# Gate weights split once: the first span stores both halves in DRAM, the other four load them

## The chip, the cores and the metric

One core of one Trainium2 chip runs the whole program. The metric is the device time of one execution in microseconds (us). The program is a hand-scheduled kernel: every engine has its own instruction stream, and semaphores tie the streams together.

## The reference

One inference step of a one-layer hybrid decoder, for 2048 prompt positions and 8 x 4 sample positions, all in float32. What bears on the change is the first half of the layer:

```
xn = rmsnorm(x, g_mix)
proj = xn @ w_in                     # 1024 x 4360
mq, mk, mv, mo, mi, mf, aq, ak, av, gt = split(proj)
h_m = mlstm(...) * sigmoid(mo)       # mo: 512 columns
h_a = sliding_window_attention(...)
ga, gb = split(sigmoid(gt))          # gt: 2048 columns
x = x + (ga * (h_m @ w_a) + gb * (h_a @ w_b)) @ w_out
```

`mo` and `gt` together are 2560 columns, which is 20 tiles of 128 columns of weights. These 20 tiles are "the gate weights" here.

## The kernel before

The program has three phases: the projection of everything that the mixers need, the mixing (`mixer_phase`, lines 462 to 1750), and the merge with the FFN (`ffn_phase`). The change lies in the mixing alone.

**What the mixing does.** It walks over 17 chunks (16 prompt chunks of 128 positions and the sample chunk, which comes first) and computes mLSTM and attention for each. These are many small, dependent operations. Between them TensorE (PE) works through the gate products: the 2080 positions are cut into 5 spans of 416 (`SPANS`, `TB`), and each span is multiplied with the 20 weight tiles (`SGN`). One such product is a *unit*; there are 100 (`GUNITS`), numbered u = 20 b + i for span b and tile i.

**A unit.** Float32 products are made of two float32r parts. The raw weight tile (128 x 1024, 512 KB) is loaded into `raw[u % 3]` (`unit_load`). ScalarE (ACT) rounds it into `wh[u % 3]` (`unit_high`, L764), VectorE (DVE) writes the residual `wl[u % 3]` (`unit_low`, L770), and PE does 24 matmuls, wh x xh, wh x xl and wl x xh for 8 row tiles, into the PSUM bank `pp[u % 2]` (`units_pe`, L829). ACT copies the bank to `gsgo[u % 2]` (`unit_act`, L750), and SyncE (SP) stores that to DRAM (`unit_store`, L639). So before the change every weight tile is loaded raw and split five times, once for each span.

**What sets the order.** PE does a unit in two halves of 12 matmuls. A fixed table, `PLACES`, says which halves stand between which pieces of a chunk: 1, 3, 1, 1, 2, 1 and 2 halves in the seven places of an ordinary chunk, so 5.5 units. ACT, DVE and SP walk the same table. All streams are in order: an instruction that waits holds back all that stand behind it.

**The waits around a unit.** PE waits for `gw_lo` (tile split) and for `g_read` (bank of unit u - 2 copied out). ACT waits, before it copies out unit u, for the store of unit u - 2 (`sg_out`), since both use the same buffer. SP issues every DMA of this phase, all on one queue:

```
def units(n, k):
    for u, h in PLACES[n][k]:
        if h == 0:
            continue
        unit_load(u + GRAWS)        # waits: tile u split
        unit_store(u - 2)           # waits: unit u - 2 copied out
```

Between these, in order, SP also loads the rows of the next chunk (`rows_load`, L606 and L607), the chunk's maxima (L615), stores the mixed rows (L674), loads the next span of x (L620), and at chunk 9 a block of loads for the phase that follows (`ahead`, L689 to L707).

Of the kernel before, what the change touches and what calls it, by code (L numbers as in the profile page):

```python
# [6 lines left out]
F32 = mybir.dt.float32  # L7
# [5 lines left out]
P = 128  # L13
D = 1024
KT = D // P
# [418 lines left out]
SGN = MO + 2 * KT  # L434
GUNITS = SPANS * SGN
GRAWS, GWS = 3, 3
# [25 lines left out]
def mixer_phase(nc, a, scratch, ctx, ev, sb, pb, next_ev):  # L462

    def wait(engine, name, count):

        if not (isinstance(count, int) and count <= 0):
            engine.wait_ge(ev(name), count)
# [1 line left out]
    N, S = CHUNKS + 1, 1  # L469
    row_of = lambda n: n - 2 if n > S else CHUNKS  # L470
    xns, prs, hhs, sgs = scratch["normed"], scratch["rows"], scratch["mixed"], scratch["gates"]
    mxs = scratch["maxima"]
    low, high = scratch["low"], scratch["high"]
    at = [0]

# [67 lines left out]
    wh = [sb(f"gwh{i}", [P, KT * P], F32R) for i in range(GWS)]  # L543
    wl = [sb(f"gwl{i}", [P, KT * P], F32R) for i in range(GWS)]
# [31 lines left out]
    def cupped(engine, n):  # L576

        if n == S:
            engine.wait_ge(ev("cup_s"), SEQS)
        else:  # L580
            wait(engine, "cup", n - 1)
# [8 lines left out]
    def _(sp):  # L590
        def rows_load(n):
            if n > N:
                return
            q = (n - 1) % 2
            wait(sp, "kw_ready", n - 2)
            wait(sp, "qk_tr", n - 2)
            cupped(sp, n - 2)
            if n == S + 2:
                sp.wait_ge(ev("sk_out"), 32)
            wait(sp, "rot_done", n - 2)  # L600
            wait(sp, "vr_ready", n - 2)
            for dst, c0, w in ((qk[q][:], 0, 512), (va[q][:, :, 0:DV], 512, 512), (ar[q][:], 1024, 776)):
                src = prs[row_of(n)][:, c0:c0 + w]
                if c0 == 512:
                    src = src.rearrange("p (h d) -> p h d", h=MH)
                sp.dma_start(dst, src).then_inc(ev(f"rows_in{q}"), 16)  # L606
            sp.dma_start(rope[q][:], a["rope"][row_of(n)]).then_inc(ev(f"rows_in{q}"), 16)  # L607
# [10 lines left out]
        def span_load(b):  # L618
            wait(sp, "gx_lo", KT * b)
            sp.dma_start(xst, xns[:, :, TB * b:TB * b + TB]).then_inc(ev("gx_in"), 16)  # L620

        def unit_load(u):
            if u >= GUNITS:
                return
            b, i = u // SGN, u % SGN
            wait(sp, "gw_lo", u - GRAWS + 1)
            dst = raw[u % GRAWS]
            if i < MO:
                sp.dma_start(dst.rearrange("p (k c) -> p k c", k=KT), a["w_mix"][:, :, C_MO + P * i:C_MO + P * i + P]
                             ).then_inc(ev(f"gw_in{u % GRAWS}"), 16)  # L630
            else:
                sp.dma_start(dst, a["w_gate"][(i - MO) // 2, (i - MO) % 2]).then_inc(ev(f"gw_in{u % GRAWS}"), 16)

        def unit_store(u):
            if u < 0:
                return
            wait(sp, "g_read", u + 1)
            done = next_ev("late_gates") if u >= GUNITS - 2 else ev(f"sg_out{u % 2}")
            sp.dma_start(sgs[u // SGN, u % SGN], kept(u)).then_inc(done, 16)  # L639

        def units(n, k):
            for u, h in PLACES[n][k]:
                if h == 0:
                    continue
                unit_load(u + GRAWS)
                unit_store(u - 2)
                if u % SGN == 4 and u // SGN + 1 < SPANS:
                    span_load(u // SGN + 1)
# [4 lines left out]
        sp.wait_ge(ev("last_rows"), 16)  # L653
        sp.dma_start(gz[:], prs[:, :, 1792:1800].rearrange("n p c -> p n c")).then_inc(ev("gz_in"), 16)
        rows_load(S)
        units(0, 0)
        sp.dma_start(sink[:], a["a_sinks"].partition_broadcast(P)).then_inc(ev("par_in"), 16)
        sp.dma_start(kc, a["cache_k"]).then_inc(ev("kc_in"), 16)
        sp.wait_ge(ev("m_ready"), 1)
        sp.dma_start(m0[0:SAMP, :], a["state_m"]).then_inc(ev("m0_in"), 16)  # L660
        units(0, 1)
        units(0, 2)
        for h in range(MH):
            r = DK * (h % 2)
# [92 lines left out]
            act.activation(xh[:, k, :], xst[:, k, :], ACT.Copy).then_inc(ev("gx_hi"), 1)  # L757

    def unit_high(act, u):
        if u >= GUNITS:  # L760
            return
        act.wait_ge(ev(f"gw_in{u % GRAWS}"), 16 * (u // GRAWS + 1))
        wait(act, "gmm", 2 * (u - GWS + 1))
        act.activation(wh[u % GWS][:], raw[u % GRAWS], ACT.Copy).then_inc(ev("gw_hi"), 1)  # L764

    def unit_low(dve, u):
        if u >= GUNITS:
            return
        wait(dve, "gw_hi", u + 1)
        dve.tensor_tensor(wl[u % GWS][:], raw[u % GRAWS], wh[u % GWS][:].bitcast(F32), ALU.subtract  # L770
                          ).then_inc(ev("gw_lo"), 1)
# [33 lines left out]
    def first_half_pe(pe, h):  # L805

        wait(pe, "gw_hi", 1)
        for w, x, ready in ((wh, xh, "gx_hi"), (wh, xl, "gx_lo"), (wl, xh, None)):
            if w is wl:
                wait(pe, "gw_lo", 1)  # L810
            for j in range(KT // 2 * h, KT // 2 * (h + 1)):
                if ready:
                    wait(pe, ready, j + 1)
                mm = pe.matmul(pp[:, 0, 0:TB], w[0][:, j * P:j * P + P], x[:, j, :],
                               start=(j == 0 and w is wh and x is xh), stop=(j == KT - 1 and w is wl))
        mm.then_inc(ev("gmm"), 1)

    def units_pe(pe, n, k):
        for u, h in PLACES[n][k]:
            if u == 0:  # L820
                first_half_pe(pe, h)
                continue
            wait(pe, "gw_lo", u + 1)
            wait(pe, "g_read", u - 1)
            for j in range(KT // 2 * h, KT // 2 * (h + 1)):
                if u % SGN == 0:
                    wait(pe, "gx_lo", KT * (u // SGN) + j + 1)
                for w, x in ((wh, xh), (wh, xl), (wl, xh)):
                    mm = pe.matmul(pp[:, u % 2, 0:TB], w[u % GWS][:, j * P:j * P + P], x[:, j, :],  # L829
                                   start=(j == 0 and w is wh and x is xh), stop=(j == KT - 1 and w is wl))  # L830
            mm.then_inc(ev("gmm"), 1)
# [845 lines left out]
    @block.scalar  # L1677
    def _(act):
        unit_high(act, 0)
        for h in range(2):  # L1680
            span_high(act, 0, h)
# [81 lines left out]
SGN = MO + 2 * KT  # L1763
# [1255 lines left out]
def build(nc, a):  # L3019

    scratch = {
        "normed": nc.dram_tensor("xn_rows", [P, KT, (CHUNKS + 1) * P], F32).ap(),
        "rows": nc.dram_tensor("proj_rows", [CHUNKS + 1, P, WROW], F32).ap(),
        "mixed": nc.dram_tensor("mixer_rows", [P, KT, SEQ + SAMP], F32).ap(),
        "maxima": nc.dram_tensor("chunk_maxima", [CHUNKS, MH * P], F32).ap(),
        "gates": nc.dram_tensor("gate_rows", [SPANS, SGN, P, TB], F32).ap(),
        "x_res": nc.dram_tensor("x_rows", [P, KT, SEQ + SAMP], F32).ap(),
        "x_norm": nc.dram_tensor("xn_ffn_rows", [P, KT, SEQ + SAMP], F32).ap(),
        "up_parts": nc.dram_tensor("up_parts", [FT, 4, 2, P, QUAD], F32).ap(),
        "down_parts": nc.dram_tensor("down_parts", [len(PARTS) * KT, 2, P, QUAD], F32).ap(),  # L3030
    }

    def events_of(tag):

        events = {}

        def ev(name):
            if name not in events:
                events[name] = nc.alloc_semaphore(tag + name)
            return events[name]  # L3040

        return ev, events

    (ev_a, all_a), (ev_m, all_m), (ev_f, _) = (events_of(t) for t in ("a_", "m_", "f_"))

    def phase(program, ev, next_ev):

        with ExitStack() as ctx:  # L3048
            program(nc, a, scratch, ctx, ev, lambda n, s, d=F32: ctx.enter_context(nc.sbuf_tensor(n, s, d)),
                    lambda n, s: ctx.enter_context(nc.psum_tensor(n, s, F32)), next_ev)  # L3050

    with ExitStack() as outer:
        for name, width in (("low", 2 * KT * TB), ("high", HIGH), ("ghd", MO)):
            scratch[name] = outer.enter_context(nc.sbuf_tensor("both_" + name, [P, width], F32))
        phase(project_phase, ev_a, ev_m)
        nc.clear_and_free_semaphores(list(all_a.values()))
        nc.all_engine_barrier()
        phase(mixer_phase, ev_m, ev_f)
        nc.clear_and_free_semaphores(list(all_m.values()))
        nc.all_engine_barrier()  # L3060
        phase(ffn_phase, ev_f, None)
# [78 lines left out]
```

## Time and profile before

| | us |
|---|---|
| median of 3 runs | 2862.28 |
| lowest and highest run | 2859.83, 2863.77 |
| the profiled execution: its own time | 2858.3 |
| the profiled execution: its span, first to last instruction | 2856.5 |
| PE matmul busy in the span | 2764.0 (97%) |
| DVE busy | 1747.3 (61%) |
| ACT busy | 1323.3 (46%) |
| HBM read, written | 415.33 MB, 152.02 MB |

The mixing runs from about 350 to 1018 us of the span. "Busy" of PE is the union of its matmuls, whose ends are modelled and overlap. The DMA share is the mean busy share of the core's 16 DMA engines; over the span they move 199 GB/s. A wait is put down to what released it.

### The profile page before, as it was taken

The numbers are of one execution on the slowest core, as the hardware profiler recorded it, in microseconds if no ns is written. First come the engines' busy times: TensorE is split into PE (matmuls) and PEld (weight loads), VectorE is DVE, ScalarE is ACT, GpSimd is POOL, SyncE is SP. The second block draws the span as 40 slices with busy tenths as digits, with TensorE's granted clock in tenths as the row PEclk, the third lists the DMA queues.
The fourth block names the chain that finished last, engine by engine and source line by source line (L and its number), as shares of the span: only waits on it lengthen the run. The fifth ranks groups of instructions, "written<-read, shape, count | busy, mean of one in ns | idle before, by whom it ended". The sixth has DMA issues, their size and how long they took to land. (4 is left out here: it accounts for less than half of the span.)

```text
span 2856.5 us, 47085 instructions
## 1 busy us (share of the span) xinstructions
PE 2764.0 (97%) x17306; PEld 2646.6 (93%) x17306; DVE 1747.3 (61%) x2752; ACT 1323.3 (46%) x2520; POOL 431.2 (15%) x663
## 2 busy tenths in 40 slices
PE   8999999999999999999989999999999999999997
PEld 8888799989998989999989999999999998999997
DVE  5212167676767668877887777856544456445554
ACT  4212235454555445555655444773443366333442
POOL 2111021211112222222200000020000003001112
PEclk9999999999999999999999999999999999999998
DMA  5534266556655458777676666767665566755654
GB/s 186 195 128 144 89 206 189 187 161 217 215 165 162 134 201 254 258 265 259 219 281 208 211 212 221 252 204 250 203 200 172 188 204 198 244 185 188 205 194 120
DMA packets 373684, 569.44 MB, mean 199 GB/s; under 512 B 50578, under 2 KB 197586, under 8 KB 373458
## 3 DMA queue, kind: packets, MB, share of 16 engines
q1 hardware_dynamic: 371346, 566.31, 60.3%
q8 instruction: 141, 2.31, 0.3%
q14 instruction: 85, 0.70, 0.1%
q10 hardware_dynamic: 2112, 0.13, 0.0%
HBM read 415.33 MB, written 152.02 MB: 199 GB/s over the span
## 5 line engine op out<-in xcount | busy, mean ns | idle before, releaser
L2376 PE MATMUL f_ps<-f_xt,f_wh 128*128 128x348 f32 (+1 forms) x3696 | 670.6, 324 | 18.8 <-DVE both_high L2805 12.0
L2376 PEld LDWEIGHTS f_ps<-f_xt,f_wh 128*128 128x128 f32 x3696 | 604.9, 190 | 25.0 <-DVE both_high L2805 16.7
L2719 DVE TENSOR_TENSOR f_wl<-both_high,f_wh 128x512 fp32r<-128x512 f32 (+1 forms) x494 | 357.1, 736 | 203.8 <-ACT f_wh L2469 200.1
L2469 ACT ACTIVATE f_wh<-both_high 128x512 fp32r<-128x512 f32 (+1 forms) x494 | 298.8, 621 | 339.6 <-PE f_ps L2381 265.2
L2376 PE MATMUL f_ps<-f_gbuf,f_wh 128*128 128x348 f32 (+1 forms) x2112 | 383.6, 322 | 14.3 <-ACT f_ps L2582 6.3
L2381 PE MATMUL f_ps<-f_xt,f_wl 128*128 128x348 f32 (+1 forms) x1848 | 371.0, 323 | 0.0
L2376 PEld LDWEIGHTS f_ps<-f_gbuf,f_wh 128*128 128x128 f32 x2112 | 342.5, 188 | 19.9 <-ACT both_low L2587 10.0
L2381 PEld LDWEIGHTS f_ps<-f_xt,f_wl 128*128 128x128 f32 x1848 | 309.3, 189 | 0.0
L829 PE MATMUL pp<-gxh,gwh 128*128 128x416 f32 x792 | 290.9, 367 | 1.5 <-DVE gxl L778 1.3
L829 PE MATMUL pp<-gxh,gwl 128*128 128x416 f32 x792 | 279.4, 353 | 0.0
L829 PE MATMUL pp<-gxl,gwh 128*128 128x416 f32 x792 | 278.1, 351 | 0.0
L2381 PE MATMUL f_ps<-f_gbuf,f_wl 128*128 128x348 f32 (+1 forms) x1056 | 214.5, 321 | 0.0
L2920 DVE TENSOR_TENSOR both_low<-f_ps,both_low 128x348 f32<-128x348 f32 (+1 forms) x224 | 114.2, 516 | 160.3 <-PE f_ps L2381 159.6
L2381 PEld LDWEIGHTS f_ps<-f_gbuf,f_wl 128*128 128x128 f32 x1056 | 176.1, 188 | 0.0
L2946 POOL TENSOR_TENSOR f_oc<-both_high,both_low 128x2 f32<-128x2 f32 (+1 forms) x176 | 52.4, 310 | 794.5 <-DVE both_high L2805 602.7
L770 DVE TENSOR_TENSOR gwl<-both_low,gwh 128x1024 fp32r<-128x1024 f32 x100 | 122.6, 1227 | 68.5 <-ACT gwh L764 68.5
L829 PEld LDWEIGHTS pp<-gxh,gwh 128*128 128x128 f32 x792 | 149.0, 188 | 15.0 <-issue 6.9
L2820 DVE SCALAR_TENSOR_TENSOR both_high<-both_high,both_low 128x696 f32<-128x696 f32 (+2 forms) x176 | 129.4, 756 | 41.3 <-ACT both_high L2596 41.2
L829 PEld LDWEIGHTS pp<-gxl,gwh 128*128 128x128 f32 x792 | 149.8, 189 | 1.6
L829 PEld LDWEIGHTS pp<-gxh,gwl 128*128 128x128 f32 x792 | 149.0, 188 | 1.6
L2596 ACT ACTIVATE both_high<-both_high,both_low 128x696 f32<-128x696 f32 (+2 forms) x176 | 137.7, 814 | 1.0 <-DVE both_high L2811 1.0
L2824 DVE SCALAR_TENSOR_TENSOR both_high<-both_high,both_low 128x696 f32<-128x696 f32 (+2 forms) x176 | 129.9, 759 | 4.7
(342 smaller groups left out, 4441.8 us busy)
## 6 DMA issues: line engine op xcount, KB each, us to landing
both_high<-in_w_up SPq DMA_DIRECT2D x220, 256.0 KB, 4.2
f_wh<-up_parts SPq DMA_DIRECT2D x176, 256.0 KB, 2.7
f_wl<-up_parts SPq DMA_DIRECT2D x176, 256.0 KB, 3.0
both_low<-in_w_gate SPq DMA_DIRECT2D x80, 512.0 KB, 4.6
up_parts<-f_wh SPq DMA_DIRECT2D x88, 256.0 KB, 2.9
up_parts<-f_wl SPq DMA_DIRECT2D x88, 256.0 KB, 3.4
both_high<-in_w_br SPq DMA_DIRECT2D x40, 512.0 KB, 4.7
both_high<-in_w_out SPq DMA_DIRECT2D x40, 512.0 KB, 4.5
```

What stands on the lines that cost most here:

```text
L770: dve.tensor_tensor(wl[u % GWS][:], raw[u % GRAWS], wh[u % GWS][:].bitcast(F32), ALU.subtract).then_inc(ev("gw_lo"), 1)
L829: mm = pe.matmul(pp[:, u % 2, 0:TB], w[u % GWS][:, j * P:j * P + P], x[:, j, :], start=(j == 0 and w is wh and x is xh), stop=(j == KT - 1 ...
L2376: pe.matmul(out, cut(wh, k), x(k), start=(start and k == 0 and x is xhi), stop=False, skip_group_check=not start or not stop)
L2381: mm = pe.matmul(out, cut(wl, k), xhi(k), start=False, stop=(stop and k == K - 1), skip_group_check=not start or not stop)
L2469: act.activation(ring_slot(wh, e, w), src, ACT.Copy).then_inc(ev("w_hi"), 1)
L2596: ins = act.activation(o, t, ACT.Identity, bias=taps[:, f, 4 * s + 3:4 * s + 4], scale=taps[:, f, 4 * s + 2:4 * s + 3])
L2719: dve.tensor_tensor(ring_slot(wl, e, w), src, ring_slot(wh, e, w).bitcast(F32), ALU.subtract).then_inc(ev("w_lo"), 1)
L2820: ins = dve.scalar_tensor_tensor(o, t, tap(1), o, ALU.mult, ALU.add)
L2824: ins = dve.scalar_tensor_tensor(o, t, tap(0), o, ALU.mult, ALU.add)
L2920: dve.tensor_tensor(t, ps[BANK[v][s]][:, 0:w], t, ALU.add).then_inc(ev(f"ps_read{BANK[v][s]}"), 1)
L2946: return pool.tensor_tensor(dst, src, unit.to_broadcast(list(src.shape)), ALU.mult)
```

## The change

In span 0 (units 0 to 19) everything is done as before, and SP also stores wh and wl of each unit, 512 KB each, to a new DRAM tensor `gate_parts` (`halves_out`). From unit 20 on there is no raw load, no rounding on ACT and no residual on DVE: SP loads both halves from `gate_parts` straight into the rings `wh` and `wl` (`halves_load`), which are still three deep. New waits: ACT's rounding of unit u from 3 to 19 waits until both halves of unit u - 3 have been stored; SP waits, before it loads unit u + 2, until PE has finished unit u - 1; PE waits on two load semaphores in place of `gw_lo`.

```diff
--- before.py
+++ after.py
@@ -469,7 +469,7 @@
     N, S = CHUNKS + 1, 1
     row_of = lambda n: n - 2 if n > S else CHUNKS
     xns, prs, hhs, sgs = scratch["normed"], scratch["rows"], scratch["mixed"], scratch["gates"]
-    mxs = scratch["maxima"]
+    mxs, gps = scratch["maxima"], scratch["gate_parts"]
     low, high = scratch["low"], scratch["high"]
     at = [0]
 
@@ -619,8 +619,28 @@
             wait(sp, "gx_lo", KT * b)
             sp.dma_start(xst, xns[:, :, TB * b:TB * b + TB]).then_inc(ev("gx_in"), 16)
 
+        def halves_out(u):
+
+            if u >= SGN:
+                return
+            sp.wait_ge(ev("gw_lo"), u + 1)
+            for j, t in enumerate((wh, wl)):
+                sp.dma_start(gps[u, j], t[u % GWS][:].bitcast(F32)).then_inc(ev(f"half_out{u % GWS}"), 16)
+
+        def halves_load(u):
+
+            if u < SGN or u >= GUNITS:
+                return
+            v = u - GWS
+            sp.wait_ge(ev("gmm"), 2 * (v + 1))
+            sp.wait_ge(ev(f"half_out{u % SGN % GWS}"), 32 * (u % SGN // GWS + 1))
+            if v < SGN:
+                sp.wait_ge(ev(f"half_out{v % GWS}"), 32 * (v // GWS + 1))
+            for j, (t, name) in enumerate(((wh, "hi_in"), (wl, "lo_in"))):
+                sp.dma_start(t[u % GWS][:].bitcast(F32), gps[u % SGN, j]).then_inc(ev(f"{name}{u % GWS}"), 16)
+
         def unit_load(u):
-            if u >= GUNITS:
+            if u >= SGN:
                 return
             b, i = u // SGN, u % SGN
             wait(sp, "gw_lo", u - GRAWS + 1)
@@ -643,6 +663,8 @@
                 if h == 0:
                     continue
                 unit_load(u + GRAWS)
+                halves_out(u + 1)
+                halves_load(u + GWS - 1)
                 unit_store(u - 2)
                 if u % SGN == 4 and u // SGN + 1 < SPANS:
                     span_load(u // SGN + 1)
@@ -653,6 +675,7 @@
         sp.wait_ge(ev("last_rows"), 16)
         sp.dma_start(gz[:], prs[:, :, 1792:1800].rearrange("n p c -> p n c")).then_inc(ev("gz_in"), 16)
         rows_load(S)
+        halves_out(0)
         units(0, 0)
         sp.dma_start(sink[:], a["a_sinks"].partition_broadcast(P)).then_inc(ev("par_in"), 16)
         sp.dma_start(kc, a["cache_k"]).then_inc(ev("kc_in"), 16)
@@ -757,14 +780,16 @@
             act.activation(xh[:, k, :], xst[:, k, :], ACT.Copy).then_inc(ev("gx_hi"), 1)
 
     def unit_high(act, u):
-        if u >= GUNITS:
+        if u >= SGN:
             return
+        if u >= GWS:
+            act.wait_ge(ev(f"half_out{u % GWS}"), 32 * (u // GWS))
         act.wait_ge(ev(f"gw_in{u % GRAWS}"), 16 * (u // GRAWS + 1))
         wait(act, "gmm", 2 * (u - GWS + 1))
         act.activation(wh[u % GWS][:], raw[u % GRAWS], ACT.Copy).then_inc(ev("gw_hi"), 1)
 
     def unit_low(dve, u):
-        if u >= GUNITS:
+        if u >= SGN:
             return
         wait(dve, "gw_hi", u + 1)
         dve.tensor_tensor(wl[u % GWS][:], raw[u % GRAWS], wh[u % GWS][:].bitcast(F32), ALU.subtract
@@ -820,7 +845,12 @@
             if u == 0:
                 first_half_pe(pe, h)
                 continue
-            wait(pe, "gw_lo", u + 1)
+            if u < SGN:
+                wait(pe, "gw_lo", u + 1)
+            else:
+                n = len([x for x in range(SGN, u + 1) if x % GWS == u % GWS])
+                pe.wait_ge(ev(f"hi_in{u % GWS}"), 16 * n)
+                pe.wait_ge(ev(f"lo_in{u % GWS}"), 16 * n)
             wait(pe, "g_read", u - 1)
             for j in range(KT // 2 * h, KT // 2 * (h + 1)):
                 if u % SGN == 0:
@@ -3026,6 +3056,7 @@
         "gates": nc.dram_tensor("gate_rows", [SPANS, SGN, P, TB], F32).ap(),
         "x_res": nc.dram_tensor("x_rows", [P, KT, SEQ + SAMP], F32).ap(),
         "x_norm": nc.dram_tensor("xn_ffn_rows", [P, KT, SEQ + SAMP], F32).ap(),
+        "gate_parts": nc.dram_tensor("gate_parts", [SGN, 2, P, KT * P], F32).ap(),
         "up_parts": nc.dram_tensor("up_parts", [FT, 4, 2, P, QUAD], F32).ap(),
         "down_parts": nc.dram_tensor("down_parts", [len(PARTS) * KT, 2, P, QUAD], F32).ap(),
     }
```

On SP, at the start of the mixing, from the raw load of unit 4 on (`in_w_mix` and `in_w_gate` are raw weight tiles, `gsgo` is a copied-out unit), there stood:

```order
L632 DMA both_low<-in_w_gate 128x1024
L657 DMA sink<-in_a_sinks 128x8
L658 DMA both_high<-in_cache_k 128x1024
L660 DMA m<-in_state_m 32x4
L632 DMA both_low<-in_w_gate 128x1024
L639 DMA gate_rows<-gsgo 128x416
```

and now:

```order
L652 DMA both_low<-in_w_gate 128x1024
L628 DMA gate_parts<-gwh 128x1024
L628 DMA gate_parts<-gwl 128x1024
L680 DMA sink<-in_a_sinks 128x8
L681 DMA both_high<-in_cache_k 128x1024
L683 DMA m<-in_state_m 32x4
L652 DMA both_low<-in_w_gate 128x1024
L628 DMA gate_parts<-gwh 128x1024
L628 DMA gate_parts<-gwl 128x1024
L659 DMA gate_rows<-gsgo 128x416
```

The two pairs of stores of halves here are those of units 2 and 3; those of units 0 and 1 stand just above, so eight stores now stand ahead of the first store of a result (`gate_rows<-gsgo`). The state, cache and row loads follow behind it as they did.

On SP in an ordinary chunk of a later span, from the load of the next chunk's rows on, there stood:

```order
L606 DMA qk<-proj_rows 128x512
L606 DMA va<-proj_rows 128x4x128
L606 DMA ar<-proj_rows 128x776
L607 DMA rope<-in_rope 128x128
L615 DMA am<-chunk_maxima 128x512
L674 DMA mixer_rows<-ht 1024x1x128
L632 DMA both_low<-in_w_gate 128x1024
L639 DMA gate_rows<-gsgo 128x416
```

and now:

```order
L606 DMA qk<-proj_rows 128x512
L606 DMA va<-proj_rows 128x4x128
L606 DMA ar<-proj_rows 128x776
L607 DMA rope<-in_rope 128x128
L615 DMA am<-chunk_maxima 128x512
L697 DMA mixer_rows<-ht 1024x1x128
L640 DMA gwh<-gate_parts 128x1024
L640 DMA gwl<-gate_parts 128x1024
L659 DMA gate_rows<-gsgo 128x416
```

One raw load for each unit has become two loads of halves. They stand directly ahead of the store of a result, as the raw load did.

## Rows read from the trace of the kernel before

**Rows 1.** the page: span; PE and the DMA engines in 40 slices
```profile
span 2856.5 us, 47085 instructions
...
PE   8999999999999999999989999999999999999997
...
DMA  5534266556655458777676666767665566755654
```

**Rows 2.** windows of the mixing: busy us per engine, PEclk, DMA share, GB/s
```profile
350.00:490.00 140.00, 135.56 (x984) 125.79 (x985) 93.81 (x228) 66.01 (x145) 24.28 (x26) 0.96 0.65 207
390.00:420.00 30.00, 29.27 (x283) 27.41 (x282) 21.16 (x72) 8.45 (x19) 6.54 (x8) 0.94 0.19 53
420.00:490.00 70.00, 68.78 (x488) 63.59 (x488) 46.54 (x86) 36.24 (x86) 8.49 (x8) 1.00 0.69 213
490.00:1000.00 510.00, 501.90 (x3479) 460.75 (x3478) 361.42 (x627) 262.18 (x603) 101.27 (x98) 1.00 0.55 176
```

**Rows 3.** rounding and residual: count, ns min/median/max, first and last start
```profile
L764 ACT ACTIVATE gwh<-both_low x100: 1040/1049/1062, 350.6 to 999.4; 128x1024 fp32r<-128x1024 f32 x100
...
L770 DVE TENSOR_TENSOR gwl<-both_low,gwh x100: 1209/1218/1599, 354.2 to 1003.1; 128x1024 fp32r<-128x1024 f32 x100
```

**Rows 4.** waits of PE, 490 to 1000 us: line, for whom, total us, times, longest us
```profile
PE p L1111 <- DVE hm L1236: 3.2, 8, 1.1
PE p L1101 <- ACT pt L1299: 1.4, 1, 1.4
PE pp L829 <- DVE gxl L778: 1.3, 2, 0.8
PE p L1040 <- DVE sm L1174: 1.3, 1, 1.3
PE p L1088 <- DVE sm L1192: 0.8, 1, 0.8
```

**Rows 5.** windows in three stretches of full queues (columns as in rows 2)
```profile
370.00:380.00 10.00, 9.79 (x61) 8.73 (x59) 6.28 (x28) 6.18 (x12) 0.00 (x0) 1.00 1.05 318
380.00:390.00 10.00, 10.00 (x79) 9.45 (x78) 5.07 (x15) 3.94 (x10) 3.40 (x4) 1.00 0.92 361
710.00:720.00 10.00, 10.00 (x71) 9.09 (x70) 7.47 (x12) 2.88 (x4) 5.59 (x7) 1.00 1.05 402
```

**Rows 6.** DMA issues, 348:1025, last row 350:390: count, KB, us to landing
```profile
both_low<-in_w_gate SPq DMA_DIRECT2D x80, 512.0 KB, 4.6
...
gate_rows<-gsgo SPq DMA_DIRECT2D x98, 208.0 KB, 3.5
...
gate_rows<-gsgo SPq DMA_DIRECT2D x5, 208.0 KB, 7.8
```

**Rows 7.** timeline, first burst: start, us, engine, line [idle before <-releaser]
```profile
362.73 0.33 SPq L639 DMA_DIRECT2D gate_rows<-gsgo  x1
...
370.60 0.52 ACT L750 ACTIVATE gsgo<-pp 128x416 f32<-128x416 f32 x1 [4.05 <-DMA gate_rows<-gsgo]
...
372.60 0.61 ACT L1254 ACTIVATE qkt<-p 128x512 f32<-128x512 f32 x1
...
373.26 0.72 PE L1014 MATMUL p<-qkt 64*128 64x128 f32 x8 [0.21 <-ACT qkt L1254]
```

**Rows 8.** timeline, second burst
```profile
442.71 0.43 SPq L639 DMA_DIRECT2D gate_rows<-gsgo  x1
...
447.68 0.52 ACT L750 ACTIVATE gsgo<-pp 128x416 f32<-128x416 f32 x1 [1.97 <-DMA gate_rows<-gsgo]
...
450.83 1.02 ACT L1299 ACTIVATE pt<-p 128x1024 f32<-128x1024 f32 x1
...
451.90 1.09 PE L1101 MATMUL p<-pt,var 128*64 128x128 f32 x16 [1.05 <-ACT pt L1299]
```

**Rows 9.** timeline, three units apart: last matmul of unit 60, first of unit 63
```profile
760.83 0.35 PE L829 MATMUL pp<-gxh,gwl 128*128 128x416 f32 x1
...
772.76 0.35 PE L829 MATMUL pp<-gxh,gwh 128*128 128x416 f32 x1
```

## The prediction

> **What bounds the kernel now.** I read the page first. PE's matmuls cover 97% of a span of 2856.5 us, and in the slices of the mixing, from the fifth to the fifteenth, its digit is 9 nearly everywhere [rows 1]. So work taken off ACT and DVE can gain only where PE stands waiting for them. The DMA engines have digits of 4 to 7 over most of the span, which looks like room. But a slice is 71 us long and hides bursts.
>
> The windows show them [rows 2]. In 490 to 1000 us (spans 1 to 4) PE is busy for 501.9 of 510.0 us and the DMA share is 0.55. In 350 to 490 us (span 0) the share is 0.65, and it is uneven: 0.19 in 390 to 420. Taking that and 420 to 490 away leaves 0.65 x 140 - 0.19 x 30 - 0.69 x 70 = 91.0 - 5.7 - 48.3 = 37.0 us busy in the 40 us from 350 to 390. There the queue is full already, as the windows of 10 us say: shares 1.05 and 0.92 at 318 and 361 GB/s [rows 5].
>
> What a full queue does to PE is in the first timeline [rows 7]. The store of unit 0's result is issued at 362.73. ACT stands idle for 4.05 us until it has landed at 370.60, since unit 2 goes into the same buffer. Behind that copy, in ACT's order, stand a rounding and the copies for the sample chunk, the last of them at 372.60, and PE's L1014 at 373.26 has waited 0.21 us for that copy. So at this place PE has no slack against the DMA queue. The second timeline is the same pattern [rows 8]: a store issued at 442.71, ACT released by it at 447.68, the copy of the attention weights at 450.83, and PE idle for 1.05 us before L1101. A rule to carry along: before asking what a change frees, ask at which places PE already hangs on the queue that the change loads.
>
> **The change, part by part.**
>
> *Rounding and residual, removed 80 times each.* 80 x 1.049 = 83.9 us of ACT and 80 x 1.218 = 97.4 us of DVE go [rows 3]. Neither engine is the bound, so the gain is at most what PE waits for them in 490 to 1000: 3.2 + 1.4 + 1.3 + 1.3 + 0.8 = 8.0 us [rows 4]. All five groups have ACT or DVE as releaser, but each waits for a chain that also holds work that stays. I take 5 us gained, with 0 and 8 as ends.
>
> *Traffic.* A pair of halves is 2 x 524,288 B = 1.05 MB. Span 0 stores 20 pairs, 21.0 MB. Spans 1 to 4 load 80 pairs, 83.9 MB, in place of 80 raw tiles, 41.9 MB. The best window moved 402 GB/s [rows 5], so I price a pair at 1.05 / 0.40 = 2.6 us of all 16 engines, and the 20 stores at 52.4 us. The Trainium skill, "DMA: Bandwidth & Descriptors", section Specifications, gives some 358 GB/s as the limit of one core against its HBM. By that page the stores would take 58.6 us and my sum would come out about 6 us higher; the 402 GB/s that this trace shows over 10 us (in rows 5) speaks against it as a ceiling, so I do not use it.
>
> *Span 0 as a whole.* The queue is busy for 91.0 us of 140. With the stores, and 1.3 us for two pairs that replace three raw tiles at the end, it is 91.0 + 52.4 + 1.3 = 144.7 us. That no longer fits, even with perfect packing, and packing is poor since SP issues in order.
>
> *First burst, 350 to 390.* Eight stores of halves now stand ahead of the store of unit 0, 4.2 MB or 10.5 us of queue. Some 3 us of room was left (40 - 37.0), so about 8 us arrive at ACT and, by rows 7, at PE. The lower end is 3 us: only the pair of unit 3 stands directly ahead of that store. The upper end is 13 us: that pair also has to wait for the split of unit 3, whose raw tile now lands one pair later. I take 8, since the row it hangs on has no slack. The later stores in this burst fall under a PE that is itself 8 us late, and the queue is nearly empty in 390 to 420 (0.19), where the backlog can drain. I cost them at nothing; if that cover is gone, the result of unit 1 is late next.
>
> *Second burst, 420 to 490.* 48.3 us busy now; ten more pairs (units 10 to 19) and the 1.3 us make 48.3 + 26.2 + 1.3 = 75.8 us in 70. So at least 5.8 us. The upper end is 16: four pairs (units 10 to 13, 10.5 us) ahead of the store in rows 8, which has no slack either, and 5.8 us after it. I take 10.
>
> *Loads of halves in spans 1 to 4.* The ring is three deep and has no raw buffer before it any more. SP may issue the pair of unit u + 2 only when PE has finished unit u - 1, so the pair has the time that PE spends on units u and u + 1. The shortest such time that I found is the one from the end of unit 60, 760.83 + 0.35 = 761.18, to 772.76: 11.6 us [rows 9]. A raw tile of 512 KB lands after 4.6 us [rows 6]; a second one adds 1.3 us of transfer, and two issues some 0.8 us, so 6.7 us. That leaves 4.9 us. A load of x for the next span (1.7 MB, 4.3 us) just fits in. The block at chunk 9 (`ahead`) does not: 4.6 MB, 11.4 us of queue, in which the share is 1.05 already [rows 5]. I take 2 us, between 0 and 8 (one such block with the whole lateness on PE).
>
> *Stores of results in spans 1 to 4.* The store of unit u - 2 stands behind the pair of unit u + 2, so it is issued when PE has finished unit u - 1, and ACT needs it landed when PE has finished u. It lands after 3.5 us [rows 6] plus 2.6 us behind the pair plus the issues: 6.9 us. A unit takes at least 24 x 0.19 = 4.5 us, so ACT stands for up to 2.4 us where two units follow each other directly, once in two chunks. Its rounding of 1.05 us is gone there. Queued behind it is the copy of the attention weights for which L1101 waits. I take 1 us in all, from 0 to 7 (1 us in each of seven pairs of chunks).
>
> *PE's new waits.* Two load semaphores in place of one: they are satisfied in advance or they are the lateness costed above. Nothing more.
>
> **Sum.** -5 + 8 + 10 + 2 + 1 = +16 us. The profiled execution took 2858.3 us, so 2874.3. It lies 4.0 us under the median of 2862.28; in medians that is 2878.3, **2878 us**, slower by 0.55%. With all terms at their low ends the sum is -8 + 3 + 5.8 = +0.8, with all at the high ends +44. They will not all fall on one side: 2864 to 2897 is this case's own range.
>
> What a measurement can tell from no change is 0.2%, 5.7 us: faster is under 2856.6, slower over 2868.0.
>
> **Rivals.**
>
> *Faster: the queue takes the stores in passing (16%).* PE does not wait for halves to be stored, only ACT's rounding three units later does, and 390 to 420 is nearly empty. If the first burst costs PE less than 1 us and the second less than 1 us, the relief of 8 us stands alone: 2862 - 8 + 1 = 2855. It decides at L1014: it holds if the store of unit 0 is not more than 1 us later than now. Against it: rows 7 and 5.
>
> *No change (13%).* The bursts cost their low ends, 3 + 5.8, and the relief is whole, 8: 2863. For it: each burst has an idle phase behind it. Against it: none of PE's lateness is given back later, since PE has no slack anywhere else.
>
> *Much slower: the loads of halves come late in every chunk (9%).* If a pair lands after 13 us in place of 6.7, PE waits 1.4 us at each tight place, about two in a chunk, for 14 chunks: 39 us, so 2878 + 39 = 2917. It decides where landing passes 11.6 us. For it: landing times of 7.8 us for mere 208 KB in the full stretch [rows 6]. Against it: a share of 0.55 becomes only 0.55 + 41.9 / 0.40 / 510 = 0.76.
>
> That the change does not do what it says can be left out: in the issued order ACT has 80 instructions fewer, and SP has 120 more, 40 stores and 160 loads for 80 raw loads.
>
> **How the numbers follow.** The forecast has 62%, of which 3% fall into "no change". So slower: 59 + 9 = 68%; same: 13 + 3 = 16%; faster: 16%. The range reaches from 2857, which leaves out the faster case but takes in no change, to 2899, which leaves out the much slower case: some 2 in 10 are outside.
>
> **What would show it.** Right: L1014, 23 us into the mixing before, comes some 8 us later, with ACT idle before its copy of unit 2 for over 10 us by a store; DMA shares over 0.9 in most of span 0, and that span 15 to 20 us longer; in spans 1 to 4 a pair of chunks takes no longer than before, L1111's wait for DVE is nearly gone, and ACT waits for stores of results in many units. Wrong: L1014 at its old time; PE waiting for `gate_parts` in every chunk; or spans 1 to 4 shorter by more than 8 us, which would mean that ACT and DVE held PE back in ways that no wait in the rows shows.

## The result, and the profile after

| | before | after |
|---|---|---|
| median | 2861.06 us (4 runs) | 2885.78 us (4 runs) |
| lowest and highest | 2858.77, 2863.77 | 2881.11, 2890.4 |
| ratio of the medians | | 1.0086, 95% interval 1.0067 to 1.0105 |
| the profiled execution | 2858.3 us | 2886.8 us |

The change costs 24.7 us in the median, and 28.5 us between the two profiled executions, on which all that follows rests. (The one after lies 1.0 us above its median, the one before 2.8 us below.)

The page of the changed kernel, its span, the granted clock and the DMA digits:

```profile
span 2885.0 us, 47053 instructions
...
PEclk9999989999999999999999999999999999999998
...
DMA  5644388777877767777576666667655556756665
```

Against [rows 1], the sixth and seventh digits of the DMA line have gone from 6 and 6 to 8 and 8, and the clock line has an 8 in the sixth slice (361 to 433 us). The windows, cut as in [rows 2] at the start of span 1 (unit 20 now starts at 516.1 in place of 489.6) and some 13 us before unit 99 (columns as there):

```profile
350.00:516.00 166.00, 143.25 (x981) 131.51 (x982) 91.06 (x225) 63.56 (x142) 22.26 (x26) 0.89 0.84 296
390.00:420.00 30.00, 29.39 (x237) 27.94 (x236) 17.77 (x67) 9.04 (x20) 5.78 (x6) 1.00 0.74 289
420.00:516.00 96.00, 85.34 (x622) 78.73 (x621) 53.86 (x108) 38.18 (x95) 12.61 (x14) 0.91 0.80 281
516.00:1029.00 513.00, 502.95 (x3480) 463.94 (x3480) 275.23 (x551) 192.37 (x526) 81.90 (x98) 0.99 0.76 255
```

390 to 420 us, nearly empty before at a share of 0.19, is at 0.74. The whole of span 0 has 0.84 in place of 0.65, and the granted clock there has fallen from 0.96 to 0.89. In spans 1 to 4 the share went from 0.55 to 0.76, as worked out in the prediction.

**Where the time went.** The 2400 matmuls of the gate units are in both traces, so the start of each unit u (its first matmul, number 24 u) can be subtracted. This table is worked out from the timelines:

| unit | start before | later by, after | what lies between this row and the one above |
|---|---|---|---|
| 2 | 364.9 | 0.1 | |
| 3 | 370.5 | 2.9 | 2.6 us of wait for `acall`, which DVE does behind two residuals |
| 4 | 378.0 | 12.5 | L1044 (L1014 before), and then a slow clock |
| 11 | 430.1 | 12.7 | |
| 15 | 457.8 | 26.5 | the second burst |
| 20 | 489.6 | 26.5 | end of span 0 |
| 46 | 661.8 | 24.7 | relief |
| 48 | 676.3 | 27.1 | two copies on ACT, which waited 3.6 and 2.5 us for stores, soon after a load of x |
| 55 | 722.0 | 26.6 | |
| 57 | 733.8 | 34.4 | the block of loads at chunk 9 |
| 99 | 1013.2 | 29.5 | relief |

Four events carry nearly all of the loss: 12.5, 13.8, 2.4 and 7.8 us. In between the difference stands still or moves in small steps: the falls add up to 7.7 us, the rises to 0.7.

A wait is only part of each event. The same stretches of work, from unit 0 to 4, 11 to 15 and 55 to 57, in the kernel before (the first number behind the comma is the time that PE was busy, the third from the end the granted clock):

```profile
352.28:378.02 25.74, 25.53 (x128) 23.35 (x129) 19.11 (x50) 14.36 (x26) 5.76 (x6) 0.88 0.93 279
430.11:457.76 27.65, 26.43 (x187) 24.12 (x186) 18.93 (x34) 14.52 (x37) 1.47 (x1) 1.00 0.74 234
721.99:733.81 11.82, 11.82 (x83) 10.92 (x82) 7.96 (x13) 6.86 (x20) 0.00 (x0) 1.00 0.77 241
```

and in the changed one:

```profile
351.90:390.49 38.59, 29.00 (x128) 25.29 (x129) 19.68 (x53) 15.19 (x28) 3.77 (x6) 0.75 0.99 335
442.81:484.27 41.46, 31.07 (x187) 28.35 (x185) 21.13 (x38) 16.35 (x39) 1.47 (x1) 0.84 0.93 334
748.59:768.19 19.60, 14.06 (x84) 12.92 (x82) 6.67 (x11) 5.88 (x19) 0.00 (x0) 0.83 0.89 329
```

PE stood idle for 9.4, 9.2 and 5.5 us more. For the same matmuls it was also busy for 3.5, 4.6 and 2.2 us more, at a granted clock of 0.75, 0.84 and 0.83 in place of 0.88, 1.00 and 1.00. So some 10 of the 34 us lost in these three events are slower work around the waits, not waits.

The waits of PE in span 0, of which the first and the third stand at the first burst, the other three at the second or just before it, at unit 12 (line, for whom, total us, times, longest):

```profile
PE p L1044 <- ACT qkt L1284: 6.5, 1, 6.5
...
PE pp L859 <- ACT gsgo L773: 5.6, 1, 5.6
...
PE p L950 <- DVE acall L882: 2.6, 1, 2.6
...
PE p L1131 <- ACT pt L1329: 2.6, 1, 2.6
PE p L1070 <- DVE ktl L1293: 2.3, 1, 2.3
```

And after it, to compare with [rows 4]:

```profile
PE p L1070 <- DVE ktl L1293: 5.5, 1, 5.5
...
PE p L1141 <- DVE hm L1266: 0.3, 1, 0.3
```

The wait for `hm`, 3.2 us before, is 0.3: that is the relief, and it comes as forecast. The first of the two rows is the event at chunk 9. Who is late there is told by ACT's waits over the whole mixing:

```profile
ACT gsgo L773 <- DMA gate_rows<-gsgo: 124.0, 35, 11.6
```

It was 20.1 us in 6 waits before. The issues (KB, median us to landing; before, the store of a result took 3.5 [rows 6]):

```profile
gwh<-gate_parts SPq DMA_DIRECT2D x80, 512.0 KB, 4.0
gwl<-gate_parts SPq DMA_DIRECT2D x80, 512.0 KB, 5.2
gate_rows<-gsgo SPq DMA_DIRECT2D x98, 208.0 KB, 5.5
```

The three bursts in the timeline, each as the issue of a store on SP, the copy on ACT that waits for that buffer, and the matmul on PE behind it. The first answers to [rows 7]:

```profile
371.14 0.51 SPq L659 DMA_DIRECT2D gate_rows<-gsgo  x1
...
380.77 0.52 ACT L773 ACTIVATE gsgo<-pp 128x416 f32<-128x416 f32 x1 [9.02 <-DMA gate_rows<-gsgo]
...
383.43 0.80 PE L1044 MATMUL p<-qkt 64*128 64x128 f32 x4 [6.47 <-ACT qkt L1284]
```

SP issues the store of unit 0 8.4 us later than before (371.14 against 362.73), with eight stores of halves ahead of it; it lands 10.2 us later, and PE's L1044 is 10.2 us later. So most of the lateness is there when the store is issued. SP is busy issuing for nearly all of that time: from 358.12 to 371.14 its timeline has 14 issues, whose rows last 12.4 us (2.1 us of waits for residuals in this stretch included), where before it had six in 3.0 us from 358.52 on. A second chain runs beside this one: the raw tiles of units 3 and 4 land at 366.94 and 370.62 in place of 363.93 and 365.46, their residuals come late on DVE, and `acall` stands behind them. Its wait of 2.6 us lies inside the 10.2 us and adds nothing to them. The second burst answers to [rows 8]:

```profile
463.12 1.30 SPq L659 DMA_DIRECT2D gate_rows<-gsgo  x1
...
469.56 0.52 ACT L773 ACTIVATE gsgo<-pp 128x416 f32<-128x416 f32 x1 [8.16 <-DMA gate_rows<-gsgo]
...
476.80 1.83 PE L1131 MATMUL p<-pt,var 128*64 128x128 f32 x16 [2.55 <-ACT pt L1329]
```

The third is chunk 9. The store of a result stands behind 4.6 MB of loads for the next phase and a pair of halves, and takes 12 us to land:

```profile
744.42 0.69 SPq L659 DMA_DIRECT2D gate_rows<-gsgo  x1
...
756.37 0.52 ACT L773 ACTIVATE gsgo<-pp 128x416 f32<-128x416 f32 x1 [10.99 <-DMA gate_rows<-gsgo]
...
758.93 0.58 PE L1070 MATMUL p<-ktr,aqt 64*128 64x256 f32 x2 [5.54 <-DVE ktl L1293]
```

Last, the windows of the first burst, with the granted clock as the third number from the end:

```profile
360.00:370.00 10.00, 9.46 (x54) 9.00 (x53) 4.31 (x8) 3.67 (x6) 2.20 (x4) 1.00 1.02 386
370.00:380.00 10.00, 4.38 (x20) 3.48 (x18) 2.26 (x5) 1.06 (x1) 0.00 (x0) 0.73 1.01 377
380.00:390.00 10.00, 6.57 (x28) 5.20 (x29) 4.84 (x23) 5.13 (x11) 0.00 (x0) 0.59 1.05 338
390.00:400.00 10.00, 10.00 (x78) 9.44 (x77) 5.25 (x20) 3.29 (x10) 0.50 (x1) 1.00 1.04 409
```

### The profile page after: what moved, and what is told of

It is laid out like the page before. It is cut to its first block and busy times, and to the rows that moved or that the text cites. A ratio compares the mean times of both kernels' runs of the same rounds, so it can differ in the third digit from the quotient of the medians.

```text
span 2885.0 us, 47053 instructions
## 1 busy us (share of the span) xinstructions
PE 2771.8 (96%) x17306; PEld 2654.3 (92%) x17306; DVE 1657.9 (57%) x2672; ACT 1250.7 (43%) x2440; POOL 408.6 (14%) x663
## 5 line engine op out<-in xcount | busy, mean ns | idle before, releaser
L2406 PE MATMUL f_ps<-f_xt,f_wh 128*128 128x348 f32 (+1 forms) x3696 | 669.0, 323 | 18.5 <-DVE both_high L2835 12.0
L2406 PEld LDWEIGHTS f_ps<-f_xt,f_wh 128*128 128x128 f32 x3696 | 603.3, 189 | 24.7 <-DVE both_high L2835 16.7
L773 ACT ACTIVATE gsgo<-pp 128x416 f32<-128x416 f32 x98 | 50.2, 513 | 209.6 <-DMA gate_rows<-gsgo 124.0
```

What stands on the lines that cost most here:

```text
L773: act.activation(kept(u), pp[:, u % 2, 0:TB], ACT.Copy).then_inc(ev("g_read"), 1)
L2406: pe.matmul(out, cut(wh, k), x(k), start=(start and k == 0 and x is xhi), stop=False, skip_group_check=not start or not stop)
```

## The experiments

Ten kernels were timed, 4 to 11 executions of each, beside the kernel before. Ratios are to the kernel before of the same call, whose medians lay between 2860.6 and 2861.5 us.

| kernel | median us | ratio (95% interval) | unit 20 later by | unit 99 later by |
|---|---|---|---|---|
| the change | 2885.8 | 1.0086 (1.0067 to 1.0105) | 26.5 | 29.5 |
| stores_only | 2883.3 | 1.0075 (1.0063 to 1.0088) | 23.3 | 23.3 |
| half_dose | 2871.7 | 1.0040 (1.0028 to 1.0053) | 10.9 | 10.9 |
| loads_only | 2863.9 | 1.0012 (1.0003 to 1.0021) | 1.3 | 2.7 |
| relief_only | 2854.0 | 0.9970 (0.9961 to 0.9980) | 1.7 | -6.2 |
| store_first | 2872.5 | 1.0044 (1.0030 to 1.0058) | 16.6 | 15.1 |
| act_queue | 2892.8 | 1.0117 (1.0100 to 1.0134) | 33.3 | 39.9 |
| more_results | 2877.7 | 1.0056 (1.0044 to 1.0069) | 25.5 | 18.5 |
| late_as_is | 2865.3 | 1.0015 (1.0006 to 1.0024) | 0.2 | 5.4 |
| late_plain | 2858.6 | 0.9994 (0.9985 to 1.0003) | 0.7 | -2.2 |
| late_stores | 2856.6 | 0.9987 (0.9978 to 0.9996) | 0.5 | -4.3 |

The last two columns come from each kernel's own profiled execution, by the units' starts as above. That of act_queue took 2900.3 us, 7.5 more than its median; the others lie within 3 us of theirs.

### stores_only: the kernel before plus the stores

```diff
 unit_load(u + GRAWS)
+halves_out(u + 1)
...
+if GWS <= u < SGN + GWS:
+    act.wait_ge(ev(f"half_out{u % GWS}"), 32 * (u // GWS))
```

> The kernel before, plus the 20 pairs of stores of halves in span 0 (and ACT's wait for them); every later span still loads raw tiles and splits them, and the stored halves are read by nobody. Theory 1 (the loss is made in span 0, by 21 MB of stores ahead of the stores of results): all of span 0's loss is here, unit 20 starts some 26 us later than before, and nothing is gained or lost after it: 2861 + 26 = 2887. Rival (the loss comes from loading twice the bytes in spans 1 to 4, and from a ring without raw buffers): at most 10 us slower than before, 2871 or less.

Measured 2883.3, 3.7 below the expectation; in its trace unit 20 is 23.3 us late, not 26, and unit 99 still 23.3. So the stores alone make a loss of nearly the whole size, in span 0 alone, and nothing is given back. The rival (loads in the later spans) falls as the main cause; that the loads cost something too, which the relief hides in the total, is the next experiment but one. The wait that the stores bring for ACT's rounding is not what costs: none of ACT's waits in the mixing of the change is put down to a store to `gate_parts`.

### half_dose: half the bytes

```diff
-for j, t in enumerate((wh, wl)):
+for j, t in enumerate((wh,)):
```

> The kernel before plus 20 stores of the rounded half alone, 10.5 MB in span 0 in place of 21. The full dose cost 22 us. Theory 1 (the queue has some room first, and past it every us of transfer becomes a us of PE; 26 us less of transfer in two bursts, of which some 12 lie in the bursts): more than half of the cost goes, 2861 + 7 = 2868 or less. Rival (each store costs what it costs, in proportion): 2861 + 11 = 2872.

Measured 2871.7, +10.2 us: the rival's number. 10.9 us in place of 23.3 in the trace, 5.2 of them in the first burst. My picture of a free first part and a steep second one was wrong; over this range each MB costs its share, here 10.9 us for 10.5 MB. PE had no room to spare in the bursts even for half. This run halves the number of SP's added issues together with the bytes, so it does not tell the two apart.

### loads_only: the change without 19 of its 20 stores

```diff
-if u >= SGN:
+if u != 10:
     return
...
-gps[u % SGN, j]
+gps[10, j]
```

> The changed kernel with one pair of halves stored (unit 10's) in place of 20, which all 80 loads of the later spans read; so four spans multiply with one weight tile, and the loads have their full size. Theory 1: span 0 is as before within 3 us; then the relief of ACT and DVE (-7 us), the block of loads at chunk 9 (+8 us) and two small waits (+2 us) as in the trace of the change: 2861 + 3 + 3 = 2864 to 2867. Rival (the loads are what costs): 2875 or more.

Measured 2863.9, as expected. In the trace: span 0 +1.3, the load of x +2.7, chunk 9 +6.6, and the relief takes 7.9 back. Doubling the bytes that the later spans load costs 9.3 us at two places, where a large transfer stands in the queue, and next to nothing elsewhere.

### relief_only: neither split nor load

```diff
 def halves_out(u):
-    if u >= SGN:
-        return
+    return
...
 def halves_load(u):
-    if u < SGN or u >= GUNITS:
-        return
+    return
```

> From unit 20 on there is no rounding, no residual and no load of any weight: PE multiplies with what the rings hold. So spans 1 to 4 compute with wrong weights; no halves are stored. It measures the relief of ACT and DVE alone, with no traffic added. Theory: the falling steps in the trace of the change add up to 7.7 us, so 2861 - 8 = 2853. Rival (ACT and DVE hold PE back more than the waits show, and the change lost that gain again to its loads): 2848 or less.

Measured 2854.0, a gain of 7.5 us, about what the falling steps in the change's trace add up to (7.7). The relief was never more than this: 181 us of work off two engines were worth the few us in which PE stood waiting for them. Of the 8.0 us of waits in [rows 4] this trace still has 1.6 (for `sm`, `gxl` and `hm`); so 6.4 us of the gain are waits that went, and no row tells what the rest was.

### store_first: the result's store ahead of the halves

```diff
 unit_load(u + GRAWS)
+unit_store(u - 2)
 halves_out(u + 1)
 halves_load(u + GWS - 1)
-unit_store(u - 2)
```

> The changed kernel with SP's order within a unit turned: the store of unit u - 2's result stands ahead of the stores and loads of halves, not behind them. Theory 1a (what counts is what stands ahead of a result's store within its own unit, and the wait for PE that holds it): ACT's waits for result stores in spans 1 to 4 nearly go and the 8 us at chunk 9 with them, span 0 loses 2.6 us less at each of its two places: 2886 - 8 - 5 = 2873. Theory 1b (the stores of earlier units fill the queue, so order within a unit matters little in span 0): only chunk 9 gains, 2878. Rival (bandwidth alone): 2884 to 2888, no change.

Measured 2872.5, theory 1a's number, but not quite by its account. Span 0 loses 9.9 us less (I had 5), chunk 9 still costs 5.6 us. Two copies on ACT in its trace, at the first burst and at chunk 9:

```profile
376.72 0.52 ACT L773 ACTIVATE gsgo<-pp 128x416 f32<-128x416 f32 x1 [5.37 <-DMA gate_rows<-gsgo]
...
741.63 0.52 ACT L773 ACTIVATE gsgo<-pp 128x416 f32<-128x416 f32 x1 [8.18 <-DMA gate_rows<-gsgo]
```

The first is 4.1 us earlier than in the change. The second still waited for 8.2 us, since the block of loads stands ahead of that store in either order.

### act_queue: the same stores from another engine's queue

```diff
-sp.dma_start(gps[u, j], ...)    # in SP's stream
+act.dma_start(gps[u, j], ...)   # in ACT's stream, behind unit_high
```

> The changed kernel with the stores of halves issued by ACT, on its own DMA queue, in place of SP; the same bytes at nearly the same times, but SP's result stores, rows and caches no longer stand behind them in one queue. Theory 1 (order in one queue): the first burst costs 3 us in place of 12.5 and the second 5 in place of 14: 2886 - 18 = 2868. Rival (16 engines are simply full, whichever queue the bytes stand in): 2880 or more, since 145 us of transfers still have to pass in 140.

Measured 2892.8, not 2868: a clear miss of my theory. One half of it did come true. The store of unit 0 is issued by SP at its old time (362.73 before) and lands at 371.53, 1.0 us later than before, where in the change it was 10.2 us late:

```profile
362.76 0.45 SPq L651 DMA_DIRECT2D gate_rows<-gsgo  x1
```

So what holds this store back in the change is SP's order. But another queue did not take the bytes out of the way. ACT's two roundings in the first burst:

```profile
375.13 1.06 ACT L786 ACTIVATE gwh<-both_low 128x1024 fp32r<-128x1024 f32 x1 [8.16 <-DMA gate_parts<-gwl]
...
383.66 1.06 ACT L786 ACTIVATE gwh<-both_low 128x1024 fp32r<-128x1024 f32 x1 [7.07 <-DMA gate_parts<-gwl]
```

They now wait 8.2 and 7.1 us for the stores of the halves themselves, since the rings are three deep; the wait has moved from the result buffer to the weight ring. PE waits there for `acall` (6.2 us) and for `qkt` (4.0 us), both behind these roundings, and unit 4 is 15.3 us late. The edit also makes ACT wait for each residual before it issues a pair, which the change does not, so it is not the queue alone that differs. In 370 to 390 us the engines are full with either queue (shares 1.01 and 1.05 in the change, 1.04 and 1.04 here). The Trainium skill, "DMA: Bandwidth & Descriptors", section "Issuing engines are not separate DMA queues", says that DMAs of all engines end on the same 16 DMA engines and interleave there; this run agrees, in that the engines are as full as before and no time was won. Its median is 7 us above the change's, with intervals that just overlap (1.0100 to 1.0134 against 1.0067 to 1.0105), so whether it is really worse stays open.

### more_results: four result buffers in spans 1 to 4

```diff
-kept = lambda u: ... sgo[u % 2]
+slot = lambda u: u % 2 if u < 20 else u % 4
+kept = lambda u: ... sgo[slot(u)] if slot(u) < 2 else raw[slot(u) - 2][:, 0:TB]
```

> The changed kernel with four result buffers from unit 20 on in place of two (the two new ones lie where raw tiles stood, which are not used any more by then); order and bytes stay. Theory 1 (in spans 1 to 4 what reaches PE is ACT standing before a buffer whose store is late): the 8 us at chunk 9 and the 2.4 us at the load of x go, span 0 keeps its 26 us: 2886 - 9 = 2877. Rival (the block at chunk 9 holds back halves or rows themselves): 2884 to 2888.

Measured 2877.7. From unit 55 to 57 the trace loses 0.9 us in place of 7.8, and from 46 to 48 0.1 in place of 2.4, while bytes and order are the same. ACT's waits for results' stores, 124.0 us in the change, are:

```profile
ACT gsgo L776 <- DMA gate_rows<-gsgo: 45.1, 10, 11.6
```

So what cost at chunk 9 was ACT standing before a buffer, with the attention copies behind it in ACT's order. The halves were late as well, but by little. Unit 56 still waits for its second half, which landed at 751.76; the profile names no releaser for such a wait:

```profile
751.85 0.42 PE L862 MATMUL pp<-gxh,gwh 128*128 128x416 f32 x1 [0.78 <-issue]
```

### late_stores, late_as_is, late_plain: store in span 1

`late_stores` stores the halves in span 1 and loads them in spans 2 to 4; raw tiles are split in spans 0 and 1.

```diff
+STORE_IN = lambda i: 1
+RAW_UNITS = [u for u in range(GUNITS) if u // SGN <= STORE_IN(u % SGN)]
+STORED_UNITS = [u for u in range(GUNITS) if u // SGN == STORE_IN(u % SGN)]
...
-if u >= SGN:
+if u not in STORED_UNITS:
```

It also has `store_first`'s order and, from unit 40 on, `more_results`' buffers. `late_plain` lacks the buffers, `late_as_is` lacks both.

> The halves are stored in span 1 in place of span 0, so raw tiles are loaded and split in spans 0 and 1 and the halves loaded in spans 2 to 4; the store of a result stands ahead of them, and from unit 40 on there are four result buffers. Theory 1 (the loss comes from adding 21 MB to the one stretch whose queue is full already): span 0 is as before, span 1, whose DMA share was about 0.55, loses 0 to 5 us, the later spans give some 5 us back and chunk 9 loses 1: 2861 + 0 to 2, at most 2864. Rival (21 MB of stores cost their 20 us wherever they stand, since PE has no slack): 2876 or more.

> late_stores without its two other edits: the halves are stored in span 1 and loaded in spans 2 to 4, but on SP they stand ahead of the store of a result as in the change, and there are two result buffers throughout. If the place of the stores alone decides span 0, the 25 us are gone here too; chunk 9 (+8) and the load of x (+2) come back: late_stores' 2857 + 9 = 2866. If more than 870 ns a unit in span 1 depended on the order, it is 2875 or more.

> late_stores with two result buffers throughout, and its order (the store of a result first). In store_first this order left 5.6 us of the loss at chunk 9, since the block of loads still stands ahead of the store there: 2857 + 5 = 2862. If the order alone were enough, 2858 or less.

Measured 2856.6, 2865.3 and 2858.6. The windows of late_stores by span (span 0, span 1, the rest):

```profile
350.00:490.00 140.00, 134.06 (x981) 124.05 (x982) 93.68 (x227) 65.57 (x144) 24.27 (x26) 0.98 0.65 211
490.00:623.00 133.00, 131.12 (x913) 120.43 (x913) 90.70 (x161) 64.36 (x152) 28.23 (x28) 1.00 0.91 328
623.00:1000.00 377.00, 374.47 (x2602) 345.23 (x2602) 206.38 (x415) 145.15 (x395) 59.55 (x71) 1.00 0.77 260
```

Span 0 is back at 0.65. Span 1 runs at a share of 0.91 and 328 GB/s, and PE loses nothing in it: unit 20 and unit 40 are both 0.5 us late (0.2 and 0.2 in late_as_is, which has the change's order). This is the clearest result of the study: the same 21 MB cost 23 us where they fall into bursts that PE hangs on, and 0 in the next span, though the queue is as full there. It is full over short stretches too. Five windows of 10 us in a row, from 500 to 550, have shares of 0.98 to 1.05 in late_as_is; together:

```profile
500.00:550.00 50.00, 48.90 (x342) 44.92 (x341) 33.33 (x57) 23.73 (x57) 11.28 (x11) 1.00 1.02 361
```

The same 50 us had a share of 0.67 in the kernel before, with PE busy for the same 48.90 us. In the whole of span 1 ACT waits for stores of results only twice, 4.9 us in all, and PE loses nothing by it. So a full queue by itself costs PE nothing; which of the differences between the spans gives span 1 its room was not tried. What follows is chunk 9: 10.1 - 1.8 = 8.3 us from unit 55 to 57 in late_as_is, 2.9 in late_plain, 1.2 in late_stores. The relief over three spans, with the rest, leaves late_stores 4.9 us faster than the kernel before, with an interval from 0.04 to 0.22% that narrowly excludes no change; it had been expected at 2861 to 2863. late_as_is came out as expected (2866). late_plain, expected at 2862, lost 2.9 us at chunk 9 in place of 5.6, and its interval takes in no change. No run gives the kernel before the new order or the new buffers. Since no wait in [rows 4] is for a result's buffer, they have little to win there, but that is argued and not measured.

## Why the prediction was right

It had 2878 us in a range from 2857 to 2899; 2885.8 was measured. Sign and mechanism held, the size was 16 us for 24.7 (28.5 in the profiled execution). By its terms, the right column from the units' starts:

| term | predicted (range) | measured |
|---|---|---|
| first burst | +8 (3 to 13) | +12.5 |
| second burst | +10 (5.8 to 16) | +13.8 |
| loads late: chunk 9 and load of x | +2 (0 to 8) | +7.8 and +2.4 |
| ACT before result buffers elsewhere | +1 (0 to 7) | +0.7 at most, in small steps |
| relief | -5 (-8 to 0) | -7.7 |
| sum | +16 | +29.5 to the last unit |

*First burst.* The chain was named with its lines, and it was that one: store of unit 0, ACT's copy of unit 2, `qkt`, L1014. The store landed 10.2 us later; the prediction had subtracted 3 us of room from 10.5 us of transfers, and no room showed. It priced the way of the store by bytes alone; 8.4 of the 10.2 us were there at the issue, while SP was working through 14 issues, for which the sum has no term. The second chain, raw tiles that land late and hold `acall`, was not named either; it stayed under the first. PE lost 2.3 us more at the lower clock level, which no term held: L1044 is 10.2 us late and unit 4, a few pieces behind it, 12.5. "The later stores I cost at nothing" held: nothing was lost from unit 4 to unit 11, while the share in 390 to 420 rose to 0.74.

*Second burst.* The same pattern, in three places: at unit 12 (3.4 us), at the bank of a unit (`pp`, a wait of 5.6 us for ACT's copy) and at the matmul of [rows 8] (2.6 us). The prediction named the last alone.

*Chunk 9.* The step that failed is "I take 2 us, between 0 and 8": it looked for halves that land late. `more_results` shows that these alone cost 0.8 us, and that what PE hung on was the store of a result behind the block. 7.8 us were lost, the high end, and with the 2.4 us at the load of x, where ACT's copies waited for stores of results too, the term lies outside its range. The prediction had that chain in span 0 and in its next term, where it priced it without the block; the two terms met at one place.

*Relief.* The bound of 8.0 us from the waits was nearly reached (7.5 in relief_only, 7.7 in the change). It was taken at 5 us because each wait's chain also holds work that stays; that work held PE back for no more than 1.6 us.

*The clock.* No term of the sum holds it. In the three large events PE was busy for 10.3 us more over the same work, at a lower granted clock (the windows under "Where the time went"). PE's added idle time in the two bursts, 9.4 and 9.2 us, is close to the 8 and 10 us that the sum took for them; what lifted them to 12.9 (counted from unit 0) and 13.8 is the slower work. So the sum is short for two reasons, this one and the term for late loads. The relief, larger than taken by 2.7 us, hides a part of it, and it is partly luck that the total came this near.

*The sum of the whole span.* The 144.7 us of transfers for 140 us gave a lower bound of 5 us, which was safe and of little use. `late_stores` has the reverse case, 0.91 busy at no cost. The sign "shares over 0.9 in most of span 0" held in 8 of 16 windows of 10 us (350 to 510).

The rivals: "the queue takes the stores in passing" needed L1014 within 1 us of its time, and it was 10 us late. "Much slower" needed halves that land after 11.6 us; they land in 4.0 and 5.2 us at the median. The forecast's sign for "ACT idle for over 10 us" came out as 9.0 us there, 11.6 at the longest.

## What to carry to other kernels

Trading compute on idle engines for bytes pays only what the busy engine waits for those engines, which one table of waits bounds; here that was 8 us, and the bytes cost more than three times that. Ask of every added transfer what stands behind it in the issuing engine's order and who hangs on that. The share of busy DMA engines does not tell: windows at 1.0 went with the loss in span 0 and with none in span 1. If a value is stored for reuse, it need not be stored the first time that it is made: here, one span later, the stores cost nothing, and with the order and the buffers mended most of the gain was kept.

## What was not expected of the hardware

- A wait of PE cost more than its length here. In the windows above, the granted clock is 0.73 in 370 to 380 and 0.59 in 380 to 390. PE had waited 2.6 us until 373.3 and worked for 1.4 us when its matmuls, 0.19 us apart at the level of 2.4 GHz, came to start 0.35 us apart, the level of 1.2 GHz. It then waited 6.5 us more, and was back at the upper level at 388.4. The pieces between L1044 and unit 4 took 2.3 us longer than before. Over all three large events the extra busy time of PE, 10.3 us, is nearly a third of the loss.
- The 16 DMA engines moved 409 GB/s in 390 to 400 us of the changed kernel with stores and loads mixed, and 386 GB/s in 360 to 370, with the three pairs of halves that SP issued from 358.1 to 364.2 under way beside loads. So windows with stores of this shape in them moved about as much as the best one with loads before (402 GB/s).
- Issues themselves took longer while the queue was full: SP's 14 issues ahead of the first store of a result fill 13.0 us, 10.9 of them without its waits for residuals, so 0.8 us each. The six before the change lasted 0.5 us each.
- Moving the same stores to a second issuing engine's queue won nothing of the 18 us that I had expected from it.
- One profiled time can mislead by some us at this size: the executions compared differ by 28.5 us, the medians by 24.7.
